# Mixture-of-experts weights on one core: every reload of gate-up weights in two halves of the contraction

## The reference

```python
for g in range(MOE_GROUPS):                      # 4 groups of 8 experts
    sl = slice(g * 8, (g + 1) * 8)
    hg = silu(einsum('nd,edf->nef', xt, w_gate[sl])) * einsum('nd,edf->nef', xt, w_up[sl])
    hg = hg * gate[:, sl, None]                  # top-1 group, top-2 experts in it
    out = out + einsum('nef,efd->nd', hg, w_down[sl])
```

## Time and profile before

| | |
|---|---|
| median of 3 runs | 1233.32 us (1232.72 to 1233.38) |
| the profiled execution, its own time | 1232.86 us |
| its span, first to last instruction | 1231.1 us |
| TensorE busy | 1095.7 us (89%), mean granted clock 0.937 |
| VectorE, ScalarE, GpSimd busy | 452.8, 228.6, 145.0 us |
| DMA | 311.96 MB, 54046 packets, mean 253 GB/s |
| first expert layer, gate-ups | 471.5 to about 694 us |
| second expert layer, gate-ups | 983.5 to about 1203.5 us |

### The profile page before, as it was taken

One profiled execution on the slowest core, in us unless ns is written; L12 is line 12 of the kernel. 1 busy time (PEld: TensorE's weight loads), 2 busy tenths in 40 slices (PEclk: granted clock), 3 DMA queues, 4 the chain that ended last, 5 costly groups with the idle time before them and its releaser, 6 DMA issues. The chain is left out here.

```text
span 1231.1 us, 14040 instructions
## 1 busy us (share of the span) xinstructions
PE 1095.7 (89%) x4918; PEld 567.0 (46%) x4918; DVE 452.8 (37%) x1165; ACT 228.6 (19%) x550; POOL 145.0 (12%) x213
## 2 busy tenths in 40 slices
PE   6999996778899997999988688899999999998884
PEld 4777775556533453333333254555564433333321
DVE  0017775674655554212211352323202632121116
ACT  0101112221300221112111132312112221121112
POOL 0000000361000001111110014041000101111100
PEclk9999997876799998999999978999999999999988
DMA  5333267000236497999999676257137689999993
GB/s 224 137 136 135 86 274 284 1 1 35 108 145 247 160 395 293 410 423 423 424 424 421 238 277 219 84 163 282 35 117 293 266 350 425 424 423 422 423 385 125
DMA packets 54046, 311.96 MB, mean 253 GB/s; under 512 B 12962, under 2 KB 13858, under 8 KB 33122
## 3 DMA queue, kind: packets, MB, share of 16 engines
q1 hardware_dynamic: 42722, 298.56, 60.8%
q0 software_dynamic: 11264, 12.61, 3.1%
HBM read 300.61 MB, written 33.59 MB: 271 GB/s over the span
## 5 line engine op out<-in xcount | busy, mean ns | idle before, releaser
L1341 PE MATMUL ps<-ring,xsT 128*64 128x512 f32 x704 | 163.7, 619 | 23.4 <-DMA ring<-in_experts 19.1
L412 PE MATMUL ps<-XT,ring 128*128 128x320 f32 x640 | 174.0, 435 | 11.4 <-DMA ring<-in_w_in 11.4
L412 PEld LDWEIGHTS ps<-XT,ring 128*128 128x128 f32 x640 | 122.4, 191 | 62.5 <-issue 12.4
L1341 PEld LDWEIGHTS ps<-ring,xsT 128*64 128x64 f32 x704 | 55.3, 142 | 129.0 <-issue 119.9
L1694 DVE TENSOR_TENSOR work<-work,ps 128x256 f32<-128x256 f32 x32 | 13.5, 421 | 269.6 <-ACT work L1423 269.6
L1368 PE MATMUL ps<-ring,hT 128*64 128x512 f32 x352 | 80.4, 598 | 1.5 <-ACT hT L1427 0.9
L1341 PE MATMUL ps<-hi,xsT 128*64 128x512 f32 x320 | 74.3, 618 | 6.9 <-DMA hi<-in_experts 6.9
L1488 POOL DMA_INDIRECT y_dram<-ys,index x32 | 32.1, 1004 | 375.1 <-DVE ys L1726 339.1
L1266 PE MATMUL ps<-C 128*128 128x512 f32 x140 | 71.5, 630 | 0.6 <-PEq L2096 0.3
L1480 POOL DMA_INDIRECT XT<-x_dram,index x32 | 32.8, 1025 | 321.4 <-DMA x_dram<-X 147.8
L1423 ACT ACTIVATE work<-ps 128x256 f32<-128x256 f32 x32 | 12.3, 384 | 274.5 <-PE ps L1341 274.5
(11 more groups left out here) (343 smaller groups left out, 1421.6 us busy)
## 6 DMA issues: line engine op xcount, KB each, us to landing
ring<-in_experts SPq DMA_DIRECT2D x36, 2048.0 KB, 24.2
ring<-in_experts SPq DMA_DIRECT2D x60, 1024.0 KB, 21.5
hi<-in_experts SPq DMA_DIRECT2D x20, 2048.0 KB, 24.3
ring<-in_w_in SPq DMA_DIRECT2D x10, 2048.0 KB, 7.8
hi<-in_experts SPq DMA_DIRECT2D x20, 1024.0 KB, 27.1
ring<-in_latent SPq DMA_DIRECT2D x60, 256.0 KB, 4.2
ring<-in_w_out SPq DMA_DIRECT2D x4, 2048.0 KB, 15.1
ring<-in_state SPq DMA_DIRECT2D x4, 1024.0 KB, 8.7
```

Source lines behind the costliest of these rows:

```text
L412: mm = pe.matmul(ps[:, q, 0:TOK], ring[:, u, k * 512 + q * P:k * 512 + (q + 1) * P], XT[:, k, :], start=(k == 0), stop=(k == KD - 1))
L1341: mm = pe.matmul(ps[e * SLOTS:(e + 1) * SLOTS, GU[p], :].rearrange("p (g f) -> p g f", g=2), xsT[:, p, k, e * SLOTS:(e + 1) * SLOTS], w[:, ...
```

## The change

Pairs 4 to 14 are now loaded in halves as well. SP waits for half of gate-up j-3 (`half_done`), issues the first halves of both experts of pair j, waits for the end of gate-up j-3, and issues the second halves. TensorE raises `half_done` half way through every gate-up and no longer only in the first. Gate-up j still waits for all of its weights before it starts (pair 15 as before for its first halves); only the number it waits for changes, since each reload now raises the semaphore twice.

```diff
                         def gate_up_pair(j):
-                            sp.wait_ge(gu_done, j - 2)
-                            for i in pair(j):
-                                load_gate_up(sp, layer, i, slot(i))
+                            for half, used in enumerate((half_done, gu_done)):
+                                sp.wait_ge(used, j - 2)
+                                for i in pair(j):
+                                    load_half_gate_up(sp, layer, i, slot(i), half)
...
                         for i in (2 * j, 2 * j + 1):
-                            halves = 16 if i >= 6 and i % RING < 2 else 0
-                            pe.wait_ge(gate_up_in[i % RING], 16 * (i // RING) + 16 + halves)
+                            pe.wait_ge(gate_up_in[i % RING], 32 * (i // RING) + 16 - (16 if j == LAST else 0))
...
-                                if j == 0 and k == KD // 2 - 1 and e == 1:
+                                if k == KD // 2 - 1 and e == 1:
                                     mm.then_inc(half_done, 1)
```

## The result

The changed kernel takes 1239.54 us (median of 4 runs, 1237.78 to 1240.94), the kernel before in the same comparison 1233.02 us. The ratio is 1.0054, 95% interval 1.0037 to 1.0072: 6.5 us slower. A second comparison gave 1238.84 us and a ratio of 1.0056 (1.0038 to 1.0073).

A forecast was written before the change was run, and what follows sets the result against it. The prediction took the full DMA weight queue to bound the expert layers. Slower 4 KB pieces (+7.6 us) and earlier issue (-1.1 us) gave +6.5 us on the median of 1233.32: 1239.8 us, range 1236.5 to 1242.5.

The forecast's parts named there:

- The sum: Whole kernel: slower pieces +7.6 us and earlier issue -1.1 us make +6.5 us, all in the expert layers.
- The bound: Late part of each expert layer: TensorE goes at the weight queue's speed, 15.8 us for a pair's weights.
- The pieces: Pairs 4 to 14, both layers: 4 KB instead of 16 KB rows slow the stream to 410 GB/s, +7.6 us.
- The earlier issue: Start of each expert layer: first halves of pair 4 issued 3.5 us earlier fill slow places, -1.1 us.
- the dip: First layer, 492 to 496 us: stream at 324 GB/s where the first reload's queue runs out; forecast to go.
- SP and the full queue: Issue of loads: SP held from the second or third changed pair on, engines don't run dry, costing nothing.
- Rival 1: Weight queue, both layers: pieces cost nothing, 410 GB/s comes from the layer's end; 1232.2 us, chance 0.16.
- Rival 2: Weight queue: SP held nearly always leaves small gaps, 3.5 us on top, 1243.3 us; chance 0.10.
- Rival 3: Halves of pairs 4 to 14 stay at the low rate of 326 GB/s, 1298 us; chance 0.02.
- rival 4: Start of layers: held SP issues first halves no earlier, 1.1 us not gained, 1240.9 us; chance 0.72 together with the forecast.
- The clock of the last gate-up: Gate-up 15 at the end of each layer: which one runs at a fallen clock is open, +-0.7 us.
- Packets: Whole execution: 16,896 packets more from the cut loads, near 70,900 in all.

The follow-up runs named there:

- the stream was taken off the path: Kernel before and changed kernel, both without the down loads of pairs 3 to 15: 1193.39 and 1194.70 us, both ratio 0.9697 to the kernel before.
- late halves: Changed kernel with both halves issued at the end of the gate-up that frees the place: 1240.38 us, ratio 1.0070 to the kernel before.
- cut whole loads: Kernel before, whole loads of pairs 4 to 14 read from a padded copy in 4 KB pieces, issued as before: 1240.86 us, ratio 1.0068.
- gate-then-up loads: Changed kernel with gate, then up, as two 1024 KB loads of 8 KB rows, both issued at the gate-up's end: 1233.93 us, ratio 1.0020.

## Why the prediction was right

*The sum.* +6.5 us was forecast and 6.5 measured, 1239.54 us against 1239.8. That it fits so closely is in part luck: by the ratios the pieces cost 8.6 us and the earlier issue gave 1.7, both more than I had, with opposite signs; and the layers alone grew by 8.7 and 9.4 us, where I had put all of the 6.5. Pair 15 starts 4.0 and 4.8 us later behind the first gate-up of its layer, not 3.

*The bound.* Right: the expert layers go at the speed of one full queue. Where the stream was taken off the path, the same change cost nothing.

*The pieces, +7.6 us.* The mechanism is right and shown from three sides: 4 KB rows in old loads cost as much, 8 KB rows in new loads a third by the ratios, and shorter rows cost more in step with their number. The size was somewhat low: late halves cost 8.6 us and cut whole loads 8.4 by the ratios, 9.8 and 10.2 in the layers of single profiles. The price of a packet, 0.46 to 0.48 ns from two short windows at the end of the layers, is 0.50 to 0.54 over pieces of 4, 2 and 1 KB (at 8 KB 0.44 by the ratio and 0.80 by the layers, too wide to say). I took it from the only stretches before with 4 KB rows and a deep queue. That windows of 6 and 7 us gave it within some 15% was luck too: moved 1 us earlier they give 0.48 and 0.55, 1 us later, towards the end of the stream, 0.73 and 0.59.

At this place stood the rule of the Trainium skill, "DMA: Bandwidth & Descriptors" (Specifications), with 512 B as the least transfer for line rate. The measurement decides against it for this use: with gate-up rows of 16 KB beside downs of 8 KB the stream had 424 GB/s, with gate-up rows of 8 KB 419, of 4 KB 412, of 2 KB 399 and of 1 KB 372. The same page's overhead of 3 cycles a packet (Why small descriptors are slow), 3.8 us by my estimate from that page, would make about half of the measured loss.

*The earlier issue, -1.1 us.* The dip nearly went, as said, and the time agrees in size (0.3 to 1.7 us), within the noise. That nothing is gained later is shown by the trace: SP is held from pair 8 on. My reason for the dip, a hole until pair 4 is issued, is not the whole of it: with the old issue and 8 KB rows in pair 3, the same windows stand at 397 to 418 GB/s in three profiles and not at 324. What the rows of pair 3 have to do with it isn't shown.

*SP and the full queue.* Right in effect, wrong in two numbers. I forecast 17 us or less from issue to landing, and it is 21 to 22. I had counted 70 to 80 packets for each engine in a full queue, and even that was added up too low, since the loads that I listed make 1,280, 80 for each engine, without the rest of pair 10; at 62.0 MB in 160 us on the weight queue, 21.8 us are 8.4 MB, more than one pair, and with 13,584 packets in that time some 115 for each engine, time held in the issue included. Nothing hung on it.

*Rivals.* Rival 1, that the number and size of loads and not the rows made 410 GB/s, is refuted by the cut copy. Rival 2, small gaps of a full queue, is refuted at its price of 3.5 us: the DMA share stays at 1.02, late halves and cut whole loads cost the same, and gate-then-up loads cost by the ratio what their packets do. Rival 3 is out. Of rival 4 only the part that I had put into the forecast came true.

*The clock of the last gate-up*, +-0.7 us: in both layers it took 8.9 us from start to end in the changed kernel, between the 8.8 and 9.5 of before.

*Packets.* 71,647 and not some 70,900: I had left out the 16 small ones of each further load.

## What to carry to other kernels

Where a queue of loads is the bound and never empty, an earlier issue buys nothing; what counts is its rate, and here the rate depended on the length of the contiguous rows all the way from 1 KB to 16 KB. Before a load is cut, look at what the cut does to the rows: lay the data out so that the part that is needed or freed first is one row; here that took back 9 us in the layers, though whole loads in the same layout were still 3 us faster. And a short window of the trace in which one kind of load runs alone gives a first price of changing all the others to that kind; move it by 1 us to see how far to trust it.

## What the runs showed of the hardware

- A packet of the weight queue costs 0.50 to 0.54 ns over the 16 engines besides its bytes (0.55 to 0.60 by the layers), some 8.5 ns on one engine, the same from 4 KB to 1 KB.
- The first loads of a queue that was empty are more sensitive to rows than a deep queue. Over the 4 us that begin 6.5 us behind the layer's first gate-up, the halves of pair 3 move with 4 KB rows at 310 to 342 GB/s in the first layer and at 350 to 364 in the second (ten profiles), with 8 KB rows at 386 to 399 and 426 to 428 (four profiles). A deep queue has 410 and 418. Long rows alone don't prevent a slow start: the dip of 324 GB/s in the kernel before holds whole loads with 16 KB rows.
- Smaller packets on the weight queue let the row transfers of GpSimd's queue through sooner: the gathers landed after 8.2 us in place of 13.9, in the same stretch of 160 us. With whole loads in 4 KB pieces it is 8.1 and in 2 KB pieces 7.0, with 8 KB rows 9.6, so it goes with the rows and not with the number of loads. Here nothing waited for them. In the kernel before:

```profile
XT<-x_dram,index POOLq DMA_INDIRECT x11, 13.9
```
